# Two ordinary products of each feed-forward replaced by seven block products, in an exact-splitting fp32 transformer kernel

## The chip, the cores and the metric

The kernel runs on one core of one Trainium2 chip. The metric is the device time in microseconds (us). Before the change three runs gave a median of 3119.59 us (3119.15 to 3120.97). The engines are called by the names of the profile: PE (TensorE) multiplies, PEld is its weight load, DVE is VectorE, ACT is ScalarE, POOL is GpSimd and SP is SyncE, which issues the weight transfers.

## The reference, cut to what matters

The program computes two transformer blocks in one launch. The change lies in the second block, which has two layers (`NL` = 2) with two feed-forwards each, so four in all, on 512 tokens plus 16 prefixed ones (`L` = 528 columns):

```python
for l in range(DEPTH_2):
    h = layer_norm(DEEPNORM_ALPHA * h + 0.5 * swiglu_ffn(h, ffn1_w13[l], ffn1_w2[l]), ...)
    mix = token_mix(h, ...)
    h = layer_norm(DEEPNORM_ALPHA * h + mix, ...)
    h = layer_norm(DEEPNORM_ALPHA * h + 0.5 * swiglu_ffn(h, ffn2_w13[l], ffn2_w2[l]), ...)
```

`swiglu_ffn` multiplies the 1024 features of `h` by a gate matrix and an up matrix, forms silu(gate) * up, and multiplies by the down matrix. The computation is in fp32. The last feed-forward needs only the 512 real tokens.

## The kernel before, in words

**Splitting.** An fp32 product is made of three fast ones: weights and activations are each split into a high half and a low half (`w_hi`, `w_lo`, `h_hi`, `h_lo`), and PE forms high x high, high x low and low x high. ACT writes the high half of a weight piece (`split_act`, line 2641), and DVE (line 2659) or POOL (line 2654) the low half, by subtraction. Raw weights come by SP's DMAs into two slots of 4096 columns; the split halves live in a ring of eight "eighths" of 512 columns.

**Tiles.** The hidden width is cut in 22 tiles (f = 0 to 21; the last a half tile), in groups of 6, 8 and 8, each followed by its share of the down product. An ordinary tile makes its gate and its up product whole: eight blocks of 128 features, three pairs, two halves of 264 columns, so 48 matmuls each and 96 a tile. A "seven" tile makes the same four block results from seven block products (Winograd's form of Strassen's scheme) of 4 x 3 = 12 matmuls of 264 columns, so 84 a tile. Its seven weight items are blocks or sums of blocks: item 0 and 5 and 1 come as they are, items 4, 3, 2 and 6 after DVE's weight sums 1 to 4 (`weight_sum_1` to `weight_sum_4`, lines 2679, 2684, 2690, 2696; the first writes the buffer `key_sum`, the others write in place). The low halves of items 0 and 5 are POOL's, the others DVE's. The matching sums of activations are made once in each feed-forward: `hidden_sums` on DVE (four subtractions over 1056 columns, lines 2787 to 2793), their high halves `t_hi` on ACT (line 2804), their low halves `t_lo` on DVE (line 2815).

**A seven tile on PE.** `seven_pe` makes the products 0 to 6 in order, called f.0 to f.6 here. Products 2, 4, 5 and 6 add into a bank that ACT has to copy out first (`kept`, line 2918, signal `sv_sb`); the copies are called kept 1, kept 3, kept 4 and kept 5, after the products whose results they take. Kept 4 stands on ACT behind the high halves of the next tile's items 1, 2 and 3, and item 2's waits for DVE's weight sum 2. The copies go to one half of `gs` or the other.

**The start of a feed-forward.** Before the change tiles 0, 1 and 2 are ordinary and 3 to 20 are sevens. PE makes tile 0's two products and tile 1's gate interleaved with the layer norm (`first_three`), then tile 1's up product, then tile 2. Tile 2's gate product waits only for ACT's silu of tile 0 (line 2991), its up product for DVE's multiplication of tile 0 (line 3085). On ACT, after the layer norm, stand eight scalings of the residual (`scale_res`, line 2608), then the `t_hi` pieces, then two weight pieces, then the silu of tile 0. On DVE stand the hidden sums, `t_lo`, two weight sums for tile 3, then the multiplication of tile 0. Each engine runs its instructions in the order written; semaphores tie the engines together.

Of the kernel before, what the change touches and what calls it, by code (L numbers as in the profile page):

```python
# [2160 lines left out]
def second_block(E):  # L2161
# [739 lines left out]
    def ffn_act(act, l, w):  # L2901
        i = w * S_FFN2
        fin = final(l, w)
        downs = [[i + 6 + 7 * sum(x in F_SEVEN for x in range(f0 + nf)) + (f0 + nf == FT) + DK * g + m for m in range(DK)]
# [63 lines left out]
        for g, (f0, nf) in enumerate(GROUPS):  # L2968
            for f in range(f0, f0 + nf):
# [17 lines left out]
                up_ps.wait(act, l, w * UP + min(2 * f + 1, UP))
                if f >= 2:
                    gl_sb.wait(act, l, n - 1)
                if f < FT - 1:  # L2990
# [830 lines left out]
```

## Time and profile before

| | us |
|---|---|
| median of three runs | 3119.59 |
| the profiled execution | 3117.75 |
| its span, first to last instruction | 3116.0 |
| PE busy | 3024.4 (97%) |
| DVE, ACT, POOL busy | 1627.7, 1139.2, 962.5 |
| mean granted clock of PE | 0.992 |

The span is what the profile divides into parts; the profiled execution took 1.75 us more than it. PE's busy time is a union of matmuls that overlap in the pipeline, so the pace of a stage is read from the chain of waits: a run of matmuls with its length divided by their number.

### The profile page before, as it was taken

How to read it: one execution, taken by the hardware profiler on the slowest of the kernel's cores; microseconds unless marked ns; L12 is line 12 of the kernel's file. 1: busy time of each engine (PE TensorE's matmuls, PEld its weight loads, DVE VectorE, ACT ScalarE, POOL GpSimd, SP SyncE). 2: the span in 40 equal slices, each digit the busy share in tenths (PEclk: the TensorE clock that was granted, in tenths of full speed). 3: DMA queues.
4: the chain of work that ended last, by engine and by line, in shares of the span. 5: the costliest groups of instructions: out<-in, count | busy, mean ns of one | idle time of the engine just before them, and what ended most of it. 6: DMA issues, size and time to landing. Idle time of an engine off the chain costs nothing.

```text
span 3116.0 us, 57215 instructions
## 1 busy us (share of the span) xinstructions
PE 3024.4 (97%) x23846; PEld 2477.9 (80%) x23846; DVE 1627.7 (52%) x2678; ACT 1139.2 (37%) x2208; POOL 962.5 (31%) x699
## 2 busy tenths in 40 slices
PE   7999999989999999999999999999999999999998
PEld 3455578644544438999999999999999999889996
DVE  3143855551122137657464468466575556376573
ACT  2041422110000017445434455356453443364453
POOL 1020266300000004332555432334332356343322
PEclk9999999999999999999999999999999999999999
DMA  7440100139999982332222122231222222113321
GB/s 320 185 169 31 55 3 3 72 139 429 428 429 429 428 350 74 109 109 75 95 82 82 55 75 103 99 112 61 95 109 102 96 82 82 55 60 117 109 75 54
DMA packets 37771, 439.02 MB, mean 141 GB/s; under 512 B 5910, under 2 KB 6678, under 8 KB 11542
## 3 DMA queue, kind: packets, MB, share of 16 engines
q1 hardware_dynamic: 36088, 434.24, 35.5%
q8 instruction: 178, 2.92, 0.4%
q10 hardware_dynamic: 1444, 1.36, 0.1%
q14 instruction: 61, 0.50, 0.0%
HBM read 432.70 MB, written 2.10 MB: 140 GB/s over the span
## 4 chain that ended last, share of the span: by engine, by line
PE 58%; ACT 3%; DVE 1%; issue 0%; DVEq 0%; ACTq 0%
PE PS L2844 23%; PE PS L2712 23%; PE PS L2709 5%; PE PS L2723 2%; PE PS L3240 2%; PE PS L2300 1%; PE PS L3275 1%; PE PS L2306 1%; PE PS L3258 1%; ACT high L2608 0%; ACT h_hi L2522 0%; ACT w_hi L2641 0%; PE PS L2313 0%; ACT low L2525 0%; ACT t_hi L2804 0%
## 5 line engine op out<-in xcount | busy, mean ns | idle before, releaser
L2654 POOL TENSOR_TENSOR w_lo<-low,w_hi 128x512 fp32r<-128x512 f32 (+4 forms) x310 | 616.7, 1995 | 1535.6 <-ACT w_hi L2641 1530.7
L2641 ACT ACTIVATE w_hi<-low 128x512 fp32r<-128x512 f32 (+3 forms) x670 | 491.6, 744 | 502.6 <-PE PS L2712 290.0
L2844 PE MATMUL PS<-t_hi,w_hi 128*128 128x264 f32 (+1 forms) x1152 | 327.1, 284 | 3.8 <-ACT low L2918 3.8
L2844 PE MATMUL PS<-t_hi,w_lo 128*128 128x264 f32 (+1 forms) x1152 | 327.6, 284 | 0.0
L2844 PE MATMUL PS<-t_lo,w_hi 128*128 128x264 f32 (+1 forms) x1152 | 326.2, 283 | 0.0
L2659 DVE TENSOR_TENSOR w_lo<-low,w_hi 128x512 fp32r<-128x512 f32 x360 | 247.0, 703 | 34.2 <-ACT w_hi L2641 33.0
L2844 PE MATMUL PS<-h_hi,w_lo 128*128 128x264 f32 (+1 forms) x864 | 244.9, 283 | 0.0
L2844 PE MATMUL PS<-h_lo,w_hi 128*128 128x264 f32 (+1 forms) x864 | 244.8, 283 | 0.0
L2844 PE MATMUL PS<-h_hi,w_hi 128*128 128x264 f32 (+1 forms) x864 | 244.3, 283 | 0.0
L2712 PE MATMUL PS<-g_hi,w_hi 128*128 128x264 f32 x1056 | 230.9, 286 | 1.2 <-DVE high L3101 1.2
L2712 PE MATMUL PS<-g_lo,w_hi 128*128 128x264 f32 x1056 | 228.6, 284 | 0.0
L1909 PE MATMUL PS<-arena 128*64 128x512 f32 x1024 | 223.1, 593 | 0.3 <-DMA arena<-wts_dram 0.3
L2844 PEld LDWEIGHTS PS<-t_hi,w_hi 128*128 128x128 f32 x1152 | 217.3, 189 | 4.8 <-ACT low L2918 4.6
L2712 PE MATMUL PS<-g_hi,w_lo 128*128 128x264 f32 x1008 | 218.6, 285 | 0.0
L2844 PEld LDWEIGHTS PS<-t_lo,w_hi 128*128 128x128 f32 x1152 | 217.3, 189 | 0.0
L2844 PEld LDWEIGHTS PS<-t_hi,w_lo 128*128 128x128 f32 x1152 | 216.8, 188 | 0.0
L3101 DVE SCALAR_TENSOR_TENSOR high<-PS,high 128x528 f32<-128x528 f32 (+1 forms) x84 | 58.7, 703 | 290.6 <-PE PS L2712 207.8
L2712 PE MATMUL PS<-h_hi,w_hi 128*128 128x264 f32 x928 | 202.9, 289 | 4.6 <-ACT low L2991 4.5
L2712 PE MATMUL PS<-h_hi,w_lo 128*128 128x264 f32 x928 | 200.0, 286 | 0.0
L2712 PE MATMUL PS<-h_lo,w_hi 128*128 128x264 f32 x928 | 199.7, 285 | 0.0
L1909 PEld LDWEIGHTS PS<-arena 128*64 128x64 f32 x1024 | 79.0, 137 | 141.3 <-issue 139.5
L2918 ACT ACTIVATE low<-PS 128x264 f32<-128x264 f32 (+1 forms) x288 | 111.4, 387 | 178.7 <-PE PS L2844 178.0
(435 smaller groups left out, 6543.5 us busy)
## 6 DMA issues: line engine op xcount, KB each, us to landing
arena<-wts_dram SPq DMA_DIRECT2D x108, 2048.0 KB, 18.2
low<-wts_dram SPq DMA_DIRECT2D x70, 2048.0 KB, 7.8
arena<-wmod_dram SPq DMA_DIRECT2D x9, 2048.0 KB, 8.1
low<-wts_dram SPq DMA_DIRECT2D x12, 1536.0 KB, 6.4
arena<-na_bias_dram SPq DMA_DIRECT2D x16, 512.0 KB, 3.6
arena<-x_dram SPq DMA_DIRECT2D x2, 2048.0 KB, 8.2
high<-tab_dram SPq DMA_DIRECT2D x1, 2225.0 KB, 25.2
low<-wts_dram SPq DMA_DIRECT2D x2, 1024.0 KB, 5.5
```

The source lines that it names most:

```text
L1909: last = nc.tensor.matmul(PS[a:b, 2 + 2 * j + half, :], xe[:, k, j * CAP:(j + 1) * CAP], w[:, x, k % 4, :], start=(k == 0), stop=(k == DK ...
L2300: mm = nc.tensor.matmul(PS[32 * j:32 * j + 32, b, at:at + QN], C[mean][:, 0:32], x[:, j * QN:(j + 1) * QN], start=first, stop=last)
L2641: nc.scalar.activation(hi, raw, ACT.Copy).then_inc(w_h.sem, 1)
L2654: nc.gpsimd.tensor_tensor(lo, raw, hi.bitcast(F32), ALU.subtract).then_inc(w_lp.sem, 1)
L2659: nc.vector.tensor_tensor(lo, raw, hi.bitcast(F32), ALU.subtract).then_inc(w_lv.sem, 1)
L2709: mm = nc.tensor.matmul(PS[:, b, :], w[wi], x[xi][:, NMETA:], **ends)
L2712: mm = nc.tensor.matmul(bank(b, h), w[wi], halves(x[xi])[:, h, :], **ends)
L2723: return nc.tensor.matmul(bank(2 * z, h), wts[z][wi][:, k * P:(k + 1) * P], part(x, h), start=first, stop=last)
L2844: last = nc.tensor.matmul(PS[:, b, 0:n], wt[wi][:, k, :], xs[xi], start=(i in (0, 1, 3) and k == 0 and j == 0), stop=(k == 3 and j == 2), ...
L2918: nc.scalar.activation(to, PS[:, 4 * (f % 2) + b, 0:width(fin)], ACT.Copy).then_inc(sv_sb.sem, 1)
L3101: nc.vector.scalar_tensor_tensor(toks(res[:, m, :], fin), sums(2 * (m % apart), fin), 0.5, toks(res[:, m, :], fin), ALU.mult, ALU.add).the ...
L3240: last = nc.tensor.matmul(PS[:, b, 0:256], (h_hi, h_lo)[xi][:, k, s:s + P], wt[wi].rearrange("p (k n) -> p k n", k=DK)[:, k, :], start=(k ...
```

## The change

Tile 2 becomes a seven, so that 19 tiles are sevens (`F_SEVEN` starts at 2). PE's work falls by 12 matmuls in each feed-forward. What goes with it:

- The order on DVE at the start of a feed-forward: weight sums 1 and 3 of the first seven tile stand ahead of the hidden sums. Weight sums 2 and 4, the low halves of tile 2's items and tile 1's multiplication come behind tile 0's.
- The order on ACT: the `t_hi` pieces come first, then items 0 and 1 of tile 2, the silu of tile 0, three of the eight scalings, the high half of tile 0's result. The other five scalings are in tiles 3, 4 (one each) and 5 (three).
- In all seven tiles ACT's silu of the first token half comes after kept 5, no longer between the next tile's items 2 and 3.
- The two halves of `gs` change roles (`kept_1`, `kept_2`), and tile 2's first product waits for the banks of tile 0, so for DVE's multiplication of tile 0 and not only for ACT's silu.

```diff
-F_SEVEN = range(3, FT - 1)
+F_SEVEN = range(2, FT - 1)
...
-    def scale_res(act, l, uu):
+    def scale_res(act, l, uu, ks=range(DK)):
         nc.scalar.drain()
-        for k in range(DK):
+        for k in ks:
             nc.scalar.activation(res[:, k, :], res[:, k, :], ACT.Identity, scale=ALPHA, bias=ashift[:, k:k + 1]).then_inc(ah_sb.sem, 1)
...
-    UP = 7
+    UP = 2 * F_SEVEN[0] + 1
+    kept_1, kept_2 = gs[:, F_SEVEN[0] % 2, :], gs[:, 1 - F_SEVEN[0] % 2, :]
...
+        def gate(f):
+            up_ps.wait(act, l, w * UP + min(2 * f + 1, UP))
+            if f >= 2:
+                gl_sb.wait(act, l, w * FT + f - 1)
+            r = slice(64, 128) if f == FT - 1 else slice(0, 128)
+            nc.scalar.activation(toks(gs[r, f % 2, :], fin), sums(4 * (f % 2), fin)[0:r.stop - r.start], ACT.Silu).then_inc(sl_sb.sem, 1)
...
             if f == F_SEVEN[0]:
+                gl_sb.wait(act, l, w * FT + f - 1)
+                kept(f, 1, kept_1[:, 0:width(fin)], 0)
+                item(f, 4)
+                gate(f - 1)
+                item(f, 5)
+                gate_copy(f - 1, f0)
                 item(f, 6)
-            elif followed:
-                second_half_gate(f - 1, f0)
-            step(0)
-            if f == F_SEVEN[0]:
-                gl_sb.wait(act, l, w * FT + f - 1)
-            kept(f, 1, gs[:, 1, 0:width(fin)], 0)
-            step(1)
-            if followed:
-                gate_copy(f - 1, f0)
-            if f == F_SEVEN[0]:
+                step(0)
                 gl_sb.wait(act, l, w * FT + f)
-            kept(f, 3, gs[:, 0, h0], 0)
+                kept(f, 3, kept_2[:, h0], 0)
+                step(1)
+            else:
+                if followed:
+                    second_half_gate(f - 1, f0)
+                step(0)
+                kept(f, 1, kept_1[:, 0:width(fin)], 0)
+                step(1)
+                if followed:
+                    gate_copy(f - 1, f0)
+                kept(f, 3, kept_2[:, h0], 0)
             step(2)
+            step(3)
+            kept(f, 4, kept_1[:, LH:LH + width(fin)], 1)
+            step(4)
+            kept(f, 5, kept_2[:, h1], 0)
             c11_sb.wait(act, l, seventh(w, f) + 1)
             nc.scalar.activation(g_full(f, f0)[:, h0], g_full(f, f0)[:, h0], ACT.Silu)
-            step(3)
-            kept(f, 4, gs[:, 1, LH:LH + width(fin)], 1)
-            step(4)
-            kept(f, 5, gs[:, 0, h1], 0)
             step(5)
+            if f in range(3, 6):
+                scale_res(act, l, 2 * w - 1, (f,) if f < 5 else range(5, DK))
             step(6)
...
                 if f == 0:
-                    scale_res(act, l, 2 * w - 1)
                     hidden_sums_high(act, l, w, fin)
-                    split_act(act, l, i + 4)
-                    split_act(act, l, i + 5)
+                    item(2, 0)
+                    item(2, 1)
                     if w == 0:
                         nc.scalar.drain()
                         act.dma_start(par, A["par"][l:l + 1, :, :].rearrange("a p n -> (a p) n")).then_inc(par_in.sem, 16)
+                    gate(0)
+                    scale_res(act, l, 2 * w - 1, range(3))
+                    gate_copy(0, f0)
+                    item(2, 2)
+                    item(2, 3)
...
                 if f == 0:
+                    weight_sum_1(dve, l, seventh(w, 2))
+                    weight_sum_3(dve, l, seventh(w, 2))
                     hidden_sums(dve, l, w, fin)
                     hidden_sums_low(dve, l, w, fin)
-                    weight_sum_1(dve, l, seventh(w, 3))
-                    weight_sum_3(dve, l, seventh(w, 3))
                 elif f == 1:
-                    low_item(3, 1)
-                    weight_sum_2(dve, l, seventh(w, 3))
-                    weight_sum_4(dve, l, seventh(w, 3))
-                elif f == 2:
-                    low_item(3, 2, 3, 4)
+                    low_item(2, 3, 4)
```

VectorE (DVE) before, from the last of the hidden sums' low halves (L2815) to tile 1's multiplication (the second L3085); L2679, L2684, L2690 and L2696 are weight sums 1, 3, 2 and 4, L2659 is an item's low half, L3023 the low half of a tile's result:

```order
L2815 TENSOR_TENSOR t_lo<-low,t_hi_7842 128x264
L2679 TENSOR_TENSOR low<-low 128x512 [waits arrived1]
L2684 TENSOR_TENSOR low<-low 128x512 [waits ks_ps0]
L3085 TENSOR_TENSOR low<-low,PS 128x528 [waits x_ps1,xt_ps0]
L3023 TENSOR_TENSOR g_lo<-low,g_hi 128x528 [waits a_ps1]
L2659 TENSOR_TENSOR w_lo<-low,w_hi 128x512 [waits qk_psd1]
L2690 TENSOR_TENSOR low<-low 128x512 [waits ks_ps0,ks_ps1]
L2696 TENSOR_TENSOR low<-low 128x512 [waits ks_ps0,qk_psd0]
L3085 TENSOR_TENSOR low<-low,PS 128x528 [waits x_ps1,xt_ps0]
```

The same stretch after the change, on to weight sum 2 of the next tile (the second L2690); L2816, L3086 and L3028 are the former L2815, L3085 and L3023:

```order
L2816 TENSOR_TENSOR t_lo<-low,t_hi_7842 128x264
L3086 TENSOR_TENSOR low<-low,PS 128x528 [waits x_ps1,xt_ps0]
L2659 TENSOR_TENSOR w_lo<-low,w_hi 128x512 [waits qk_psd1]
L2690 TENSOR_TENSOR low<-low 128x512 [waits ks_ps0,ks_ps1]
L3028 TENSOR_TENSOR g_lo<-low,g_hi 128x528 [waits a_ps1]
L2696 TENSOR_TENSOR low<-low 128x512 [waits ks_ps0,qk_psd0]
L2659 TENSOR_TENSOR w_lo<-low,w_hi 128x512 [waits qk_psd1] x3
L3086 TENSOR_TENSOR low<-low,PS 128x528 [waits x_ps1,xt_ps0]
L2679 TENSOR_TENSOR low<-low 128x512 [waits ks_ps0,qk_psd0,arrived1]
L3028 TENSOR_TENSOR g_lo<-low,g_hi 128x528 [waits a_ps1]
L2659 TENSOR_TENSOR w_lo<-low,w_hi 128x512 [waits qk_psd1]
L2684 TENSOR_TENSOR low<-low 128x512 [waits ks_ps0]
```

The first two weight sums have left this stretch for the place ahead of the hidden sums; the next tile's weight sums 1 and 3 have entered it, since the next tile now follows one tile earlier.

ScalarE (ACT) before, from the end of the layer norm (L2582) to the high half of tile 0's result (L2913); L2608 is a scaling, L2804 a `t_hi` piece, L2641 an item's high half, L2991 the silu of tile 0 with its table load:

```order
L2582 ACTIVATE low<-high 128x8
L2608 ACTIVATE high<-high,low 128x528 x8
L2804 ACTIVATE t_hi_7842<-low 128x1056 [waits d_ps1] x2
L2804 ACTIVATE t_hi_7843<-low 128x1056 [waits d_ps1]
L2804 ACTIVATE t_hi_7843<-low 128x792 [waits d_ps1]
L2804 ACTIVATE t_hi_7842<-low 128x264
L2641 ACTIVATE w_hi<-low 128x1024 [waits xt_ps0,arrived1] x2
L2981 DMA high<-par_dram 128x890
L2991 ACT_TABLE_LOAD
L2991 ACTIVATE low<-PS 128x528 [waits xt_ps0]
L2913 ACTIVATE g_hi<-low 128x528 [waits x_ps0]
```

The same stretch after (L2805, L2997, L2930 and L2914 are the former L2804, L2981, L2991 and L2913):

```order
L2582 ACTIVATE low<-high 128x8
L2805 ACTIVATE t_hi_7842<-low 128x1056 [waits d_ps1] x2
L2805 ACTIVATE t_hi_7843<-low 128x1056 [waits d_ps1]
L2805 ACTIVATE t_hi_7843<-low 128x792 [waits d_ps1]
L2805 ACTIVATE t_hi_7842<-low 128x264
L2641 ACTIVATE w_hi<-low 128x512 [waits xt_ps0,arrived1] x2
L2997 DMA high<-par_dram 128x890
L2930 ACT_TABLE_LOAD
L2930 ACTIVATE low<-PS 128x528 [waits xt_ps0]
L2608 ACTIVATE high<-high,low 128x528 x3
L2914 ACTIVATE g_hi<-low 128x528 [waits x_ps0]
```

The eight scalings have left the head of the stretch; three stand behind the silu. The DMA is only in the first feed-forward of each layer.

## Rows read from the trace of the kernel before

**Rows 1.** The page: busy us (share of the span) and instructions by engine.

```profile
PE 3024.4 (97%) x23846; PEld 2477.9 (80%) x23846; DVE 1627.7 (52%) x2678; ACT 1139.2 (37%) x2208; POOL 962.5 (31%) x699
```

**Rows 2.** PE's waits, 1190 to 3050 us: total us, times, longest us.

```profile
PE PS L2712 <- ACT low L2991: 4.5, 2, 2.5
PE PS L2844 <- ACT low L2918: 3.8, 4, 1.4
...
PE PS L2709 <- ACT low L2991: 2.6, 1, 2.6
```

**Rows 3.** Chain, layer 0's second feed-forward: start us, us, what.

```profile
1802.03 11.96 PE PS L2712 x96
...
1822.66 23.66 PE PS L2844 x192
```

**Rows 4.** The same view, group 2 of that feed-forward.

```profile
1881.33 81.89 PE PS L2844 x672
```

**Rows 5.** The same view, layer 0's first feed-forward.

```profile
1200.21 17.62 PE PS L2712 x144
...
1225.88 14.14 PE PS L2844 x114
```

**Rows 6.** The same view, layer 1's first feed-forward.

```profile
2169.01 13.49 PE PS L2712 x96
...
2190.57 23.68 PE PS L2844 x192
```

**Rows 7.** The same view, layer 1's second feed-forward.

```profile
2766.43 12.94 PE PS L2709 x48
...
2787.35 23.00 PE PS L2844 x192
```

**Rows 8.** VectorE's timeline, as rows 3: start us, us, instruction, [idle before].

```profile
1789.95 1.26 DVE L2787 TENSOR_TENSOR low<-low 128x1056 f32<-128x1056 f32 x1 [2.95 <-POOL h_lo L2590]
...
1795.18 6.98 DVE L2815 TENSOR_TENSOR t_lo<-low,t_hi 128x1056 fp32r<-128x1056 f32 x5
1802.09 2.88 DVE L2679 TENSOR_TENSOR low<-low 128x512 f32<-128x512 f32 x1
```

**Rows 9.** VectorE's timeline, tile 3 of the same feed-forward.

```profile
1814.82 0.70 DVE L3085 TENSOR_TENSOR low<-low,PS 128x528 f32<-128x528 f32 x1
1815.43 1.19 DVE L2679 TENSOR_TENSOR low<-low 128x512 f32<-128x512 f32 x1
...
1818.26 0.68 DVE L2659 TENSOR_TENSOR w_lo<-low,w_hi 128x512 fp32r<-128x512 f32 x1
```

**Rows 10.** GpSimd's (POOL's) timeline, the same feed-forward, 1786 to 1826 us.

```profile
1785.83 4.09 POOL L2590 TENSOR_TENSOR h_lo<-low,h_hi 128x264 fp32r<-128x264 f32 x5
1799.09 5.33 POOL L2654 TENSOR_TENSOR w_lo<-low,w_hi 128x1024 fp32r<-128x1024 f32 x2 [9.17 <-ACT w_hi L2641]
...
1814.78 3.00 POOL L2654 TENSOR_TENSOR w_lo<-low,w_hi 128x512 fp32r<-128x512 f32 x2 [5.90 <-ACT w_hi L2641]
```

**Rows 11.** ScalarE's timeline, the same feed-forward.

```profile
1793.98 4.09 ACT L2804 ACTIVATE t_hi<-low 128x1056 fp32r<-128x1056 f32 x5
...
1799.98 1.28 ACT L2991 ACT_TABLE_LOAD   x1
...
1821.72 0.61 ACT L2641 ACTIVATE w_hi<-low 128x512 fp32r<-128x512 f32 x1
1822.23 0.37 ACT L2918 ACTIVATE low<-PS 128x264 f32<-128x264 f32 x1
```

**Rows 12.** Windows: stretch, its us, busy (x) by engine, clock (PEclk), DMA share, GB/s.

```profile
2169.60:2173.10 3.50, 3.50 (x19) 3.50 (x18) 3.21 (x3) 0.23 (x1) 1.35 (x1) 0.51 0.02 5
```

**Rows 13.** First hidden sum on VectorE in the other three feed-forwards (timeline).

```profile
1192.01 1.26 DVE L2787 TENSOR_TENSOR low<-low 128x1056 f32<-128x1056 f32 x1 [2.95 <-POOL h_lo L2590]
...
2156.51 1.26 DVE L2787 TENSOR_TENSOR low<-low 128x1056 f32<-128x1056 f32 x1 [2.94 <-POOL h_lo L2590]
...
2754.47 1.22 DVE L2787 TENSOR_TENSOR low<-low 128x1024 f32<-128x1024 f32 x1 [2.95 <-POOL h_lo L2590]
```

More of the change, by code:

```diff
@@ L2136 @@
             for c in range(nf // 2):
-                add_chunk([x for f in (f0 + 2 * c, f0 + 2 * c + 1) for x in ([SINGLE] * 2 if f < 3 else [SEVEN] if f in F_SEVEN else [HALF_TILE])])
+                add_chunk([x for f in (f0 + 2 * c, f0 + 2 * c + 1) for x in ([SINGLE] * 2 if f < F_SEVEN[0] else [SEVEN] if f in F_SEVEN else [HALF_TILE])])
             for c in range(DNC):
@@ L2148 @@
 NS = len(PIECES)
-S_FFN = 6 + 7 * NSEVEN + 1 + DK * len(GROUPS)
+S_FFN = 2 * F_SEVEN[0] + 7 * NSEVEN + 1 + DK * len(GROUPS)
 S_MIX = S_FFN
@@ L2871, in ffn_pe @@
                     last.then_inc(up_ps.sem, 1)
-                i += 2 if f < 3 else 1
+                i += 2 if f < F_SEVEN[0] else 1
             ending = g == len(GROUPS) - 1
@@ L2903, in ffn_act @@
         fin = final(l, w)
-        downs = [[i + 6 + 7 * sum(x in F_SEVEN for x in range(f0 + nf)) + (f0 + nf == FT) + DK * g + m for m in range(DK)]
+        downs = [[i + 2 * F_SEVEN[0] + 7 * sum(x in F_SEVEN for x in range(f0 + nf)) + (f0 + nf == FT) + DK * g + m for m in range(DK)]
                  for g, (f0, nf) in enumerate(GROUPS)]
@@ L2981, in ffn_act @@
                         act.dma_start(par, A["par"][l:l + 1, :, :].rearrange("a p n -> (a p) n")).then_inc(par_in.sem, 16)
-                elif f == 1:
-                    item(3, 0)
-                    item(3, 1)
+                    gate(0)
[3 more added lines that the diff above has]
+                    item(2, 3)
                 elif f == FT - 1:
                     split_act(act, l, downs[g][2])
[L2987 to L2990, printed above, removed]
-                    nc.scalar.activation(toks(gs[:, f % 2, :], fin), sums(4 * (f % 2), fin), ACT.Silu).then_inc(sl_sb.sem, 1)
-                else:
-                    nc.scalar.activation(toks(gs[64:128, f % 2, :], fin), sums(4, fin)[0:64], ACT.Silu).then_inc(sl_sb.sem, 1)
-                if f == 2:
-                    item(3, 4)
-                    item(3, 5)
-                if f != 2:
+                    gate(f)
                     gate_copy(f, f0)
-                if f == 1:
-                    item(3, 2)
-                    item(3, 3)
             for x in range(4 if g < len(GROUPS) - 1 else 3, DK):
@@ L3089, in ffn_dve @@
                     nc.vector.tensor_tensor(toks(x[64:128], fin), toks(x[64:128], fin), sums(4, fin)[64:128], ALU.mult).then_inc(g_sb.sem, 1)
-                if f != 2:
+                if f == 0:
+                    low_item(2, 1)
+                    weight_sum_2(dve, l, seventh(w, 2))
+                    gate_low(f, f0)
+                    weight_sum_4(dve, l, seventh(w, 2))
+                    low_item(2, 2)
+                elif f == FT - 1:
                     gate_low(f, f0)
@@ L3187, in second_block @@
             if g == 0:
-                last_product += [(up_ps, w * UP + z + 1) for z in range(6)]
+                last_product += [(up_ps, w * UP + z + 1) for z in range(2 * F_SEVEN[0])]
             last_product += [(sv_ps, 7 * seventh(w, f) + x + 1) for f in range(f0, f0 + nf) if f in F_SEVEN for x in range(7)]
```

8 lines of the change are left out of this document (4 added, 4 removed).

## The prediction, made before the changed kernel ran

> **What bounds the kernel now.** I read the busy line first: PE is busy for 97% of the span [rows 1], so a change pays where it takes matmuls away without making PE wait. The chain of waits then gives PE's true pace. In a stretch without waits 672 matmuls take 81.89 us [rows 4], 0.122 us each, so a seven tile of 84 takes 10.24 us, one of its block products of 12 takes 1.46 us, and an ordinary tile of 96 takes 11.7 us (measured 11.96 with its start [rows 3]). The list of PE's waits shows where PE stands in the feed-forwards. It waits three times for the silu of tile 0 (line 2991), before tile 2: 2.0 and 2.5 us, and 2.6 us in the last feed-forward [rows 2]; layer 0's first has no such wait, since there 144 matmuls run through [rows 5]. And it waits four times, 3.8 us in all, for a copy of line 2918: kept 4 of tile 3, the first seven tile [rows 2]. Everything the change touches lies between those two waits. The timelines of DVE, ACT and POOL there give the durations.
>
> **What is removed.** 12 matmuls in each of four feed-forwards: 12 x 0.122 = 1.46 us each, 5.8 us in all. If nothing else changed, this would be the gain. ACT's eight scalings no longer delay the silu of tile 0; the load of the table and the silu follow the `t_hi` pieces and two weight pieces. Before, ACT ended `t_hi` at 1798.07 [rows 11]; now `t_hi` waits for DVE's sums instead and ends at about 1797.1, and with two pieces of 0.6 us in place of two of 1 us, then 1.28 for the table and 0.6 for the silu, tile 0's silu is ready at 1800.0 instead of 1801.9. But tile 2's first product also needs the bank that DVE's multiplication of tile 0 reads, and that is now the later one.
>
> **The path through DVE, in the second feed-forward of layer 0.**
> 1. DVE sat idle for 2.95 us before the hidden sums, waiting for POOL's `h_lo` pieces [rows 8]. Weight sums 1 and 3 of tile 2 (0.68 us each, as the DVE instruction of the same width in rows 9) go into this hole. They don't come free. Where POOL runs, DVE instructions whose two inputs both lie in SBUF take longer: weight sum 1 of 0.68 us took 1.19 while POOL worked from 1814.78, and 2.88 beside POOL's two wide pieces, ending half a microsecond after one of them ended; the multiplication that reads PSUM took its usual 0.70 in the same place [rows 8 to 10]. So DVE and POOL take turns, and POOL's remaining `h_lo` pieces (4.09 / 5 = 0.8 each) come out late by what the two sums insert beyond POOL's gaps. I take 0.6 us; the ends are 0 and 1.4 (both sums in full). The hidden sums start at 1790.55.
> 2. The four hidden sums take 5.23 us to the start of `t_lo` (1795.18 - 1789.95). `t_lo` took 6.98 [rows 8] with a wait for a wide POOL piece inside; at the hidden sums' pace (1.26 for 1056 columns) it is 5.0 alone. POOL's piece there is now item 0 of tile 2, 1.3 us (3.00 / 2 less its own wait), so 1.2 us of waiting (ends 0 and 1.3). `t_lo` ends at about 1801.8, the multiplication of tile 0 (0.70) at 1802.4, and PE starts tile 2 at 1802.5. Before it was 1802.03. PE's wait grows to 2.5 us.
> 3. From there DVE has no idle time. Until it reaches weight sum 2 of tile 3 it has eight instructions at a pitch of 0.60 (low half of item 1, weight sum 2, tile 0's low half, weight sum 4, three low halves, multiplication of tile 1), to 1807.2; weight sum 1 of tile 3 beside POOL's item 5, 1.3 instead of 0.6; tile 1's low half, 0.6; item 6 beside POOL's item 0 of tile 3, 1.7 instead of 0.6; weight sum 3, item 1, weight sum 2, together 1.9. Sum: 1812.6. Waits of 0.7 and 1.1 for POOL are in it.
> 4. ACT then makes the high halves of items 2 and 3 (0.61, pitch 0.52) and kept 4 (0.37) [rows 11]: 1812.6 + 1.45 = 1814.05. PE starts product 2.5 at 1814.1. Left alone PE would be there at 1802.5 + 5 x 1.46 = 1809.8. It waits 0.1 for item 2's low half, 1.2 for kept 3 (behind the wait for `gs`, 1809.5), and 3.1 for kept 4.
> 5. From 2.5 on PE has two products of tile 2 and tiles 3, 4, 5. Before, the stretch that began at 1822.66 had two products of tile 3 and tiles 4, 5 [rows 3]. So the change of the end is 1814.1 + 10.24 - 1822.66 = +1.7 us. In other words: 1.46 us of matmuls saved, tile 2 begun 0.5 later, and 4.3 us of waiting inside the first seven tile against 1.4 before.
>
> In tile 3 weight sum 2 of tile 4 comes some 4.9 us after the tile's start and kept 4 after 6.4, where PE asks for it after 7.3, so I expect no more waits. The silu moved behind kept 5 helps here by 0.3 and has no other price. The scalings in tiles 3 and 4, one each, of about the 0.6 us of a high half [rows 11], lie beside matmuls. The three in tile 5 delay its high half by about 0.2 us, ahead of the 60 matmuls of the down product that don't need tile 5. SP's next transfer into the slot of tiles 2 and 3 is let go by that chunk's last low half, now no later than before. The other groups keep their order.
>
> **The other feed-forwards**, by the start of the hidden sums [rows 13]. Layer 1's first: same schedule, 366.56 later, 2.5 starts at 2180.7, against 2190.57 [rows 6]: +0.3 (before, it already held a slow stretch, below). Layer 1's second, 964.52 later, 256 columns, so shorter by 0.3 and a tile of 9.96: +0.9 against 2787.35 [rows 7]. Layer 0's first: DVE's multiplication is ready at 1204.4, before PE gets to tile 2 at 1206.1 (48 of the 144 matmuls [rows 5]), so there is no first wait; DVE's path loses about 0.6 where it needs kept 1; 2.5 starts at 1216.8, against 1225.88: +1.1. Sum of the four: +4.0 us.
>
> **The clock.** Where PE waited 2.5 us the granted clock fell to 0.51 from 0.6 us after it resumed, for 3.5 us [rows 12], that is to the 1.2 GHz level; the 96 matmuls then took 13.49 instead of 11.96 [rows 6, 3], so 1.5 us more. After the wait of 2.6 it fell too (12.94 for 48 matmuls of 512 columns [rows 7]); after that of 2.0 it didn't. The new first wait (2.5, three times) may bring it down, but its price goes into the wait for kept 4: 0.35 us at most, 0.5 in all. The new wait for kept 4 is 2.7 to 3.4 us, four times, and behind it PE sets the pace: each fall costs 1.6. I take two of four: 3.3 us. Ends: 0 and 6.4.
>
> The sum is 4.0 + 0.5 + 3.3 = +7.8 us on the profiled execution's 3117.75 us, so 3125.6. The median of the runs is 1.84 above that execution: 3127.4 us.
>
> The Trainium skill, SBUF — State Buffer, section "Who interferes with whom", says that a VectorE instruction with two SBUF inputs contends with a GpSimd instruction that reads SBUF, and that one with at most one such input does not. By that rule, the trace agrees (1.19 against 0.68, and 0.70 for the PSUM reader). It speaks against putting the weight sums beside `h_lo`.
>
> **Rivals.**
> - *Faster: POOL waits, not DVE.* If DVE held the port in back-to-back runs, the 3.6 us of waits in steps 1 to 3 would be gone: 2.5 would start at 1810.5, -1.9 us in this feed-forward, and -3.3, -2.6 and -0.7 in the others, together -8.5: 3111.1. Against it stand rows 8 and 10, where POOL got in between two DVE instructions; for it, that my places for POOL's pieces are estimates. 8%.
> - *The clock holds.* The schedule is right, and the longer waits bring no slow stretch: +4.0 to +4.5, 3123.9. For it: one of the three waits before left the clock up. With partly shorter DVE waits the time comes to lie nearer 3119. Together 32%.
> - *The forecast*, waits and two or three slow stretches: 3125 to 3130. 45%.
> - *DVE stays late into tile 3.* If every turn with POOL costs a full piece of 1.3 us, the path is 1.6 longer in each feed-forward, and kept 4 of tile 3 is waited for as well: +6.4 more, 3133.8. 13%.
> - *Tile 5's three scalings delay the down product.* They would have to eat the slack of 60 matmuls, 7.3 us less some 4 for tile 5's result; from 3 us of lateness on it would cost what goes beyond. 2%, in the range above.
>
> Of this kernel a measurement can tell about 0.2% (6.2 us) from no change: under 3113.4 is faster, over 3125.8 slower. Faster 0.09, the same 0.38, slower 0.53. The range of eight in ten is 3115 to 3134: it leaves out the first rival and the worst of the fourth. The forecast alone would be 3123 to 3130.
>
> **What the profile after would show.** Step 2: PE waits for DVE line 3086, not for ACT's silu, about 2.5 us, before tile 2 in three feed-forwards, and not at all in the first. Step 3: VectorE without idle time from tile 0's multiplication to weight sum 2, and weight sums beside POOL's pieces at 1.2 us and more. Step 4: PE's largest wait is for line 2919 (kept 4 of tile 2), 2.7 to 3.4 us each, 12 to 17 us for that line in all with kept 3, against 3.8 before. Step 5: stretches of 276 matmuls (2.5 to the end of tile 5) starting 8 to 10 us earlier than 1822.66 and its likes. The clock: slow stretches within 1 us after these waits. The prediction is wrong if that line's waits sum to less than 8 us (then the time is below 3119), or if the hidden sums start at the old time.

## The result, and the profile after

The changed kernel took 3127.46 us (median of nine runs, 3124.97 to 3132.75), the kernel before 3118.72 (nine runs, 3115.59 to 3120.97): the ratio is 1.0035, with a 95% interval of 1.0026 to 1.0043, so slower by more than 0.2%. (The ratio is estimated over all the runs; the quotient of the two medians, 1.0028, lies inside the interval.) The prediction said 3127.4 us with slower as the likeliest outcome. The profiled execution took 3126.33 us, its span 3123.4 us at a mean clock of 0.991.

The page's busy line, which answers to [rows 1]: PE's busy time fell by 3.4 us, and DVE's rose by 43.

```profile
PE 3021.0 (97%) x23846; PEld 2476.0 (79%) x23846; DVE 1670.6 (53%) x2726; ACT 1160.5 (37%) x2248; POOL 964.3 (31%) x699
```

The number of matmuls is the same as before. Three feed-forwards have 12 fewer each, but in the last one, with its 512 tokens, 48 matmuls over 512 columns became 84 over 256, which is the work of 42. So there too an eighth of the tile's work is saved, but not 12 instructions.

PE's waits from 1190 to 3060 us, as in [rows 2] (total us, times, longest us):

```profile
PE PS L2845 <- ACT low L2919: 14.1, 7, 2.9
PE PS L2845 <- issue: 4.9, 2, 2.4
...
PE PS L2845 <- DVE low L3086: 2.8, 1, 2.8
```

Line 2919 is `kept`. Its 14.1 us are four waits of 2.75 to 2.93 us for kept 4 of tile 2, and three of 0.66, 0.99 and 1.02 for kept 3; before, this line's waits came to 3.8 us. The two waits put down to "issue" and the one for L3086 are the same wait, before tile 2: DVE's multiplication of tile 0 ended at 1802.35 and PE started at 1802.45. The silu of tile 0 (ended at 1800.09) is waited for no more.

The chain of waits in layer 0's second feed-forward, with [rows 3] (start us, us, what):

```profile
1787.67 2.91 POOL h_lo L2590 x3
1790.60 1.26 DVE low L2788
...
1795.91 4.24 DVE t_lo L2816 x3
...
1801.74 0.61 DVE low L3086
...
1807.20 1.37 DVE low L2679
...
1809.19 1.68 DVE w_lo L2659
...
1812.00 0.69 DVE low L2690
...
1813.33 0.61 ACT w_hi L2641
1813.94 0.29 ACT low L2919
1814.27 35.41 PE PS L2845 x276
```

For the 27 us shown no step of the chain is PE's: POOL's last `h_lo` pieces, then DVE's list from the hidden sums to weight sum 2 (L2690), then ACT, then product 2.5. The timelines give the durations. VectorE's, which answers to [rows 8, 9]:

```profile
1786.95 1.12 DVE L2679 TENSOR_TENSOR low<-low 128x512 f32<-128x512 f32 x1
1788.10 1.13 DVE L2684 TENSOR_TENSOR low<-low 128x512 f32<-128x512 f32 x1
1790.60 1.26 DVE L2788 TENSOR_TENSOR low<-low 128x1056 f32<-128x1056 f32 x1 [1.36 <-POOL h_lo L2590]
...
1795.82 5.92 DVE L2816 TENSOR_TENSOR t_lo<-low,t_hi 128x1056 fp32r<-128x1056 f32 x5
1801.66 0.69 DVE L3086 TENSOR_TENSOR low<-low,PS 128x528 f32<-128x528 f32 x1
...
1807.12 1.45 DVE L2679 TENSOR_TENSOR low<-low 128x512 f32<-128x512 f32 x1
1808.49 0.69 DVE L3028 TENSOR_TENSOR g_lo<-low,g_hi 128x528 fp32r<-128x528 f32 x1
1809.11 1.76 DVE L2659 TENSOR_TENSOR w_lo<-low,w_hi 128x512 fp32r<-128x512 f32 x1
...
1812.00 0.68 DVE L2690 TENSOR_TENSOR low<-low 128x512 f32<-128x512 f32 x1
```

And GpSimd's, with [rows 10]:

```profile
1786.76 3.80 POOL L2590 TENSOR_TENSOR h_lo<-low,h_hi 128x264 fp32r<-128x264 f32 x4 [0.15 <-ACT low L2525]
1797.72 1.67 POOL L2654 TENSOR_TENSOR w_lo<-low,w_hi 128x512 fp32r<-128x512 f32 x1 [7.16 <-ACT w_hi L2641]
1806.72 1.30 POOL L2654 TENSOR_TENSOR w_lo<-low,w_hi 128x512 fp32r<-128x512 f32 x1 [7.34 <-ACT w_hi L2641]
1809.00 1.32 POOL L2654 TENSOR_TENSOR w_lo<-low,w_hi 128x512 fp32r<-128x512 f32 x1 [0.98 <-ACT w_hi L2641]
```

Each of the last three POOL pieces lies beside DVE work that is longer than usual: `t_lo` by 1.1 us (e7 below gives its length alone), weight sum 1 by 0.8 and the low half by 1.1 over the 0.68 of their width. In the last two, DVE's instruction ends 0.55 us after POOL's piece. The first two weight sums, beside `h_lo`, are longer by 0.44. From the start of the hidden sums to weight sum 2 nothing else in DVE's list is longer.

The stretches from product 2.5 to the end of tile 5 in the other three feed-forwards (chain of waits; [rows 5 to 7]):

```profile
1215.62 33.89 PE PS L2845 x276
...
2184.15 35.30 PE PS L2845 x276
...
2783.66 34.45 PE PS L2845 x276
```

In the first three feed-forwards the same 276 matmuls take 33.89 or 35.3 to 35.4 us, and the clock tells them apart. Windows (stretch, its us, busy (x) by engine, clock, DMA share, GB/s): the first around the start of product 2.5 in layer 1's first feed-forward, the second from 0.4 us after that start in layer 0's first:

```profile
2183.90:2187.30 3.40, 3.15 (x14) 3.15 (x15) 2.38 (x6) 1.89 (x6) 1.50 (x1) 0.50 0.01 2
1216.00:1219.50 3.50, 3.50 (x32) 3.50 (x30) 3.39 (x7) 2.48 (x7) 1.52 (x1) 1.00 0.00 0
```

The first row is a slow stretch: 3.4 us at a granted clock of 0.50, the 1.2 GHz level. The second holds 32 matmuls at the full clock, where the first has 14.

Where the time went, counted in each feed-forward from the end of the layer norm on DVE to the end of tile 5 on PE:

| feed-forward | start of 2.5 after the norm | change of tile 5's end | of it a slow stretch |
|---|---|---|---|
| layer 0, first | 27.24 | +0.68 | none |
| layer 0, second | 27.24 | +3.33 | 1.52 |
| layer 1, first | 27.24 | +1.86 | 1.41 |
| layer 1, second | 26.92 | +2.55 | 1.39 |

The slow stretches are priced as 35.41 and 35.30 less 33.89, and the last as 34.45 less 33.06 (276 at the pace of [rows 7]). The sum is +8.4: 4.1 from the schedule and 4.3 from three slow stretches behind 2.5. The span grew by 7.4; the part ahead of these feed-forwards and the part behind tile 5 of the last came out 1.0 shorter in this pair of profiles.

From the end of tile 5 to the end of the last seven tile the first three feed-forwards take 235.3 us before and after alike. So the silu moved behind kept 5 in all sevens, and the three scalings in tile 5, cost nothing that these profiles show.

### The profile page after: what moved, and what is told of

Read it like the earlier page. It is cut to its first block, busy times and chain, and to the rows that moved or that the text cites. A ratio compares the mean times of both kernels' runs of the same rounds, so it can differ in the third digit from the quotient of the medians.

```text
span 3123.4 us, 57359 instructions
## 1 busy us (share of the span) xinstructions
PE 3021.0 (97%) x23846; PEld 2476.0 (79%) x23846; DVE 1670.6 (53%) x2726; ACT 1160.5 (37%) x2248; POOL 964.3 (31%) x699
## 3 DMA queue, kind: packets, MB, share of 16 engines
q1 hardware_dynamic: 36088, 434.24, 35.4%
## 4 chain that ended last, share of the span: by engine, by line
PE 57%; DVE 3%; ACT 1%; issue 0%; POOL 0%; DVEq 0%; ACTq 0%
PE PS L2845 24%; PE PS L2712 21%; PE PS L2709 4%; PE PS L3247 2%; PE PS L2723 1%; PE PS L2300 1%; PE PS L3282 1%; DVE t_lo L2816 1%; PE PS L2306 1%; DVE w_lo L2659 1%; PE PS L3265 1%; ACT h_hi L2522 1%; ACT low L2525 0%; POOL h_lo L2590 0%; PE PS L2313 0%
## 5 line engine op out<-in xcount | busy, mean ns | idle before, releaser
L2641 ACT ACTIVATE w_hi<-low 128x512 fp32r<-128x512 f32 (+3 forms) x690 | 494.6, 735 | 474.6 <-PE PS L2712 286.9
L2845 PE MATMUL PS<-t_hi,w_hi 128*128 128x264 f32 (+1 forms) x1216 | 346.5, 285 | 14.1 <-ACT low L2919 14.1
L2845 PE MATMUL PS<-t_hi,w_lo 128*128 128x264 f32 (+1 forms) x1216 | 346.9, 285 | 0.0
L2845 PE MATMUL PS<-t_lo,w_hi 128*128 128x264 f32 (+1 forms) x1216 | 345.5, 284 | 0.0
L2659 DVE TENSOR_TENSOR w_lo<-low,w_hi 128x512 fp32r<-128x512 f32 x380 | 273.5, 737 | 27.9 <-ACT w_hi L2641 27.1
L2845 PE MATMUL PS<-h_hi,w_hi 128*128 128x264 f32 (+1 forms) x912 | 260.0, 285 | 7.7 <-issue 4.9
L2845 PE MATMUL PS<-h_lo,w_hi 128*128 128x264 f32 (+1 forms) x912 | 260.1, 285 | 0.0
L2845 PE MATMUL PS<-h_hi,w_lo 128*128 128x264 f32 (+1 forms) x912 | 260.0, 285 | 0.0
L2919 ACT ACTIVATE low<-PS 128x264 f32<-128x264 f32 (+1 forms) x304 | 118.0, 388 | 197.2 <-PE PS L2845 193.0
L2712 PE MATMUL PS<-h_hi,w_hi 128*128 128x264 f32 x832 | 182.5, 288 | 0.2
L2845 PEld LDWEIGHTS PS<-h_hi,w_hi 128*128 128x128 f32 x912 | 173.5, 190 | 8.6 <-issue 8.5
L2712 PE MATMUL PS<-h_hi,w_lo 128*128 128x264 f32 x832 | 179.7, 285 | 0.0
```

What stands on the lines that cost most here:

```text
L2641: nc.scalar.activation(hi, raw, ACT.Copy).then_inc(w_h.sem, 1)
L2659: nc.vector.tensor_tensor(lo, raw, hi.bitcast(F32), ALU.subtract).then_inc(w_lv.sem, 1)
L2712: mm = nc.tensor.matmul(bank(b, h), w[wi], halves(x[xi])[:, h, :], **ends)
L2845: last = nc.tensor.matmul(PS[:, b, 0:n], wt[wi][:, k, :], xs[xi], start=(i in (0, 1, 3) and k == 0 and j == 0), stop=(k == 3 and j == 2), ...
L2919: nc.scalar.activation(to, PS[:, 4 * (f % 2) + b, 0:width(fin)], ACT.Copy).then_inc(sv_sb.sem, 1)
```

## The experiments

The theory: the path to product 2.5 is DVE's list with its turns against POOL, then kept 4, which stands on ACT behind weight sum 2; each long wait may also lower PE's clock. The kernel before ran beside each group of experiments, with medians of 3116.4 to 3116.6 us, 2 us less than beside the change, so the ratios are compared: the change stands at 1.0035. The line numbers move a little with each edit; `kept` is L2918 in the kernel before, L2919 in the changed one, L2920 in e12. Starts are counted from the end of the layer norm on DVE, as in the table above. A trace shows one execution of a kernel, and so does each count of slow stretches.

**e1: ACT's scalings alone, in the kernel before.** Three of the eight behind tile 0's silu, one each in tiles 3 and 4, three in tile 5.

```diff
...
+            if f in range(3, 6):
+                scale_res(act, l, 2 * w - 1, (f,) if f < 5 else range(5, DK))
...
                 if f == 0:
-                    scale_res(act, l, 2 * w - 1)
                     hidden_sums_high(act, l, w, fin)
...
+                if f == 0:
+                    scale_res(act, l, 2 * w - 1, range(3))
```

> The kernel before (tile 2 still ordinary) with only the scalings moved: three behind the silu of tile 0, one each in tiles 3 and 4, three in tile 5. Theory (a DVE path with turns against POOL sets the changed kernel's start): here tile 2's first product needs only ACT's silu, which comes at 1800.3 instead of 1801.9 in layer 0's second feed-forward, so PE's three waits of 2.0, 2.5 and 2.6 us before tile 2 shrink to 0.5 or less, and the two slow stretches behind them go: 1.6 to 2 us and 1.5 us of clock twice, some 8 us less than before, 3110 to 3113. The wait for kept 4 of tile 3 stays (3 to 5 us in all). Rival (the moved scalings are themselves a cost, since ACT is late in tiles 3 to 5): no gain or a loss, 3118 to 3123, and more waits for line 2918. Second rival: DVE is what tile 2 really waits for here too (its second product needs the multiplication of tile 0 at 1806.3): the wait moves to DVE and the gain is below 3 us.

Measured: 3118.64 us, ratio 1.0008 [0.9999, 1.0017]. PE's waits:

```profile
PE PS L2844 <- ACT low L2918: 7.5, 6, 2.0
...
PE PS L2712 <- POOL w_lo L2654: 2.1, 2, 1.1
PE PS L2709 <- POOL w_lo L2654: 1.4, 1, 1.4
```

The expectation of a gain missed. In three feed-forwards the wait before tile 2 fell by 1.0 to 1.4 us, and PE now waited for POOL's low half; but the wait for kept 4 of tile 3 grew to 1.93 to 2.01 us, and behind each of these three waits came a slow stretch of 3.4 us. In layer 0's second feed-forward product 3.5 began 35.68 us after the norm, where it began at 35.65 before: weight sum 2 of tile 4 came no earlier. An earlier start of PE is only waiting moved one tile on when DVE's list is the limit.

**e2: the change with all eight scalings at the head of ACT's list again.**

```diff
-            if f in range(3, 6):
-                scale_res(act, l, 2 * w - 1, (f,) if f < 5 else range(5, DK))
...
                 if f == 0:
+                    scale_res(act, l, 2 * w - 1)
                     hidden_sums_high(act, l, w, fin)
...
-                    scale_res(act, l, 2 * w - 1, range(3))
```

> The changed kernel with all eight scalings back at the head of ACT, ahead of the t_hi pieces. Theory: the silu of tile 0 then comes at 1801.1 to 1801.6, still before DVE begins the multiplication of tile 0 at 1801.7, so PE's waits stay as they are (22 us for tiles 2's start and kept 4 together, 2.5 starts within 0.3 us of where it was): within 2 us of the changed kernel, 3125 to 3130. Rival (ACT's order carries the start): tile 2 starts 1 to 2 us later in three feed-forwards and the time is 4 us or more above the changed kernel, over 3131.

Measured: 3127.12 us, ratio 1.0031 [1.0019, 1.0043], as expected, the wait for kept 4 and kept 3 again 14.1 us in 7. In three feed-forwards product 2.5 began within 0.04 us of the table's times. In the change the place of the scalings is worth nothing.

In layer 0's first feed-forward 2.5 began at 28.34, 1.1 us later. There PE came to tile 2 at 17.1 us after the norm, as in the kernel before, and not at 16.0 as in the changed kernel's profile: the last slow stretch before it lasted 10.2 us and not 6.8. Kept 1 waited for PE, the high half behind it for kept 1, and DVE for that high half (ACT's and DVE's timelines):

```profile
1207.90 0.39 ACT L2919 ACTIVATE low<-PS 128x264 f32<-128x264 f32 x1 [0.98 <-PE PS L2845]
1208.84 0.69 DVE L2659 TENSOR_TENSOR w_lo<-low,w_hi 128x512 fp32r<-128x512 f32 x1 [0.77 <-ACT w_hi L2641]
```

**e3: weight sums 1 and 3 behind the hidden sums and `t_lo`.**

```diff
-                    weight_sum_1(dve, l, seventh(w, 2))
-                    weight_sum_3(dve, l, seventh(w, 2))
                     hidden_sums(dve, l, w, fin)
                     hidden_sums_low(dve, l, w, fin)
+                    weight_sum_1(dve, l, seventh(w, 2))
+                    weight_sum_3(dve, l, seventh(w, 2))
```

> The changed kernel with weight sums 1 and 3 of tile 2 behind the hidden sums' low halves, as before the change. Theory: the hidden sums start 0.65 us earlier, the two sums then cost 1.2 us of the path: the multiplication of tile 0 and product 2.5 come 0.5 to 0.6 us later in three feed-forwards and 1.0 to 1.2 in layer 0's first, where the early sums cost nothing; some 3 us more than the changed kernel, 3128 to 3133. Rival (the turns with POOL beside h_lo cost more than the sums give): 2.5 starts earlier and the time falls below 3126.

Measured: 3131.56 us, ratio 1.0047 [1.0033, 1.0060], as expected; the interval overlaps that of the change, so the traces have to tell. PE waits 3.16, 3.16 and 3.52 us before tile 2, and product 2.5 comes 0.7 to 1.6 us later in the four feed-forwards. So the hole in front of the hidden sums is the better place for the two sums, although they don't come free there.

**e4: kept 4 and kept 5 of tile 2 ahead of the high halves on ACT.**

```diff
+            if f == F_SEVEN[0]:
+                kept(f, 4, kept_1[:, LH:LH + width(fin)], 1)
+                kept(f, 5, kept_2[:, h1], 0)
             step(2)
             step(3)
-            kept(f, 4, kept_1[:, LH:LH + width(fin)], 1)
+            if not (f == F_SEVEN[0]):
+                kept(f, 4, kept_1[:, LH:LH + width(fin)], 1)
...
```

> The changed kernel with ACT's kept 4 and kept 5 of tile 2 ahead of the high halves of tile 3's items 2, 3 and 4, so that product 2.5 no longer hangs on weight sum 2 of tile 3. Theory: the wait of 2.9 us before 2.5 goes in all four feed-forwards (2.5 starts at 1811.4 instead of 1814.3), but DVE is late with everything, so a wait of about 2 us comes back before 3.5, where kept 4 of tile 3 hangs on weight sum 2 of tile 4; net 0.8 us each plus one or two fewer slow stretches: 3 to 6 us less than the changed kernel, 3121 to 3125. Rival (the wait was ACT's order alone and DVE has slack): no new wait at 3.5, 2.9 us each and three slow stretches gained, 3110 to 3113.

Measured: 3120.18 us, ratio 1.0012 [1.0003, 1.0021], 0.8 us below the expected range. PE's waits:

```profile
PE PS L2845 <- ACT low L2919: 10.0, 11, 1.3
PE PS L2845 <- issue: 4.9, 2, 2.4
```

The waits of 2.9 us before 2.5 are gone (kept 3's of 0.7 to 1.0 stay), 1.0 to 1.25 us and 0.7 us came in tile 3, and only one slow stretch is left in the four feed-forwards, behind a wait before tile 2. So the wait was the copy's place behind weight sum 2; about two thirds of it came back a tile later.

**e5: the same in tiles 2 and 3.** The condition is `f < F_SEVEN[0] + 2`.

> As e4_kept45_tile2, with kept 4 and kept 5 of tile 3 ahead of tile 4's items too. e4 left per feed-forward a wait of 2.4 before tile 2 (three times), 1.0 in tile 2 and 1.2 + 0.7 in tile 3. Theory (DVE is late with everything in the first sevens, and ACT's order passes that on): the 1.9 in tile 3 goes and at most 1 of it comes back in tile 4, so 4 to 6 us less than e4: 3114 to 3117. Rival (kept 4 and 5 before the items put the items late instead): waits for low halves of items (DVE line 2659) in tile 4, no gain on e4, 3119 or more.

Measured: 3124.50 us, ratio 1.0021 [1.0012, 1.0031]; the expectation missed, and it is no better than e4. PE's waits for `kept` are 12.4 us in 16. ACT's timeline in tile 3 to 4:

```profile
1821.93 0.64 ACT L2914 ACTIVATE g_hi<-high 128x528 fp32r<-128x528 f32 x1 [2.94 <-DVE high L3038]
1822.48 0.65 ACT L2919 ACTIVATE low<-PS 128x264 f32<-128x264 f32 x2
```

Kept 4 and kept 5 of tile 3 (L2919) now stand behind the high half of tile 2's result (L2914), which waits 2.94 us for DVE (L3038). Here the copy that was freed from one wait for DVE stood behind another.

**e6: weight sum 2 of tile 3 two instructions earlier on DVE.**

```diff
             elif f == F_SEVEN[0]:
                 gate_low(f - 1, f0)
+                weight_sum_3(dve, l, s + 1)
+                weight_sum_2(dve, l, s + 1)
                 low_item(f, 6)
-            if not alone:
+                low_item(f + 1, 1)
+            if not alone and f != F_SEVEN[0]:
                 weight_sum_3(dve, l, s + 1)
                 low_item(f + 1, 1)
...
```

> The changed kernel with one order changed on DVE: in tile 2 weight sums 3 and 2 of tile 3 come ahead of item 6 of tile 2 and item 1 of tile 3. Nothing is taken away. Theory (the path to product 2.5 runs through DVE's list to weight sum 2): that list is two instructions shorter, one of which stood beside a POOL piece, and the POOL piece now delays weight sum 3 instead: 2.5 starts 1.2 us earlier (1813.0 in layer 0's second feed-forward), the wait before it is 1.6 to 1.8 instead of 2.9, fewer slow stretches: 4 to 8 us less than the changed kernel, 3119 to 3123. Rival (the wait belongs to PE's late start or to ACT): 2.5 starts where it did, 3125 to 3128.

Measured: 3120.92 us, ratio 1.0018 [1.0009, 1.0027], as expected. In layer 0's second feed-forward the wait before 2.5 fell from 2.88 to 1.87 us, with PE's start of tile 2 unchanged at 15.43 us after the norm (`kept` 9.2 us in 6). Nothing was taken away, and 2.5 came 1.0 us earlier there, 0.4 to 0.7 in the others. This shows that weight sum 2 sets kept 4, and so 2.5.

**e7: POOL only writes.** POOL's subtractions for items 0 and 5 of tile 2 and item 0 of tile 3 are replaced by a fill with zeros of the same buffers.

```diff
+        if PIECES[i % NS][4] in [(w * NSEVEN, 0) for w in range(2)] + [(w * NSEVEN, 5) for w in range(2)] + [(w * NSEVEN + 1, 0) for w in range(2)]:
+            nc.gpsimd.memset(lo.bitcast(F32), 0.0).then_inc(w_lp.sem, 1)
+            return
```

> The changed kernel, but POOL fills three low halves of each feed-forward with zeros in place of the subtraction: items 0 and 5 of tile 2 and item 0 of tile 3. That part of the computation is left out. POOL then reads nothing there. Theory (DVE instructions with two SBUF inputs take turns with POOL's reading): the last pieces of t_lo, weight sum 1 of tile 3 and item 6 of tile 2 take 1.25, 0.68 and 0.68 us instead of 2.34, 1.45 and 1.76; tile 2 starts 1.1 us and product 2.5 some 2.9 us earlier in three feed-forwards and 1 to 2 in the first; with one or no slow stretch left, 9 to 14 us less than the changed kernel, 3113 to 3118. Rival (they take long for another reason, such as data just written by ACT): durations stay, 3125 to 3128.

Measured: 3112.86 us, ratio 0.9990 [0.9981, 0.9999], 0.1 us below the expected range. VectorE's timeline:

```profile
1792.26 4.83 DVE L2819 TENSOR_TENSOR t_lo<-low,t_hi 128x1056 fp32r<-128x1056 f32 x5
...
1802.82 0.68 DVE L2682 TENSOR_TENSOR low<-low 128x512 f32<-128x512 f32 x1
...
1804.23 0.69 DVE L2662 TENSOR_TENSOR w_lo<-low,w_hi 128x512 fp32r<-128x512 f32 x1
```

And GpSimd's:

```profile
1794.14 0.53 POOL L2655 MEMSET w_lo<- 128x512 f32 x1 [7.14 <-ACT w_hi L2641]
```

`t_lo` takes 4.83 us in place of 5.92, weight sum 1 0.68 in place of 1.45, the low half 0.69 in place of 1.76: 1.1, 0.8 and 1.1, the waits for POOL of steps 2 and 3. That is 3.0 us less, but weight sum 2 of tile 3 ends only 2.4 us earlier (23.3 us after the norm instead of 25.7), since DVE now waits 0.26 us for the high half of tile 0's result and stands idle in smaller gaps. So 2.5 comes 1.9 to 2.4 us earlier, not 2.9. PE's first wait becomes 1.3 to 1.7 us, the one before 2.5 1.7, and no slow stretch is left there, where the changed kernel had four. The fills stand in the same places of POOL's list; the first and the third lay beside DVE instructions with two SBUF inputs, and these took their usual time.

**e8: DVE's multiplication of tile 0 ahead of the last `t_lo` piece.** The fourth piece moves behind weight sum 2 of tile 2.

```diff
...
-                    hidden_sums_low(dve, l, w, fin)
+                    hidden_sums_low(dve, l, w, fin, range(3))
...
                     low_item(2, 1)
                     weight_sum_2(dve, l, seventh(w, 2))
+                    hidden_sums_low(dve, l, w, fin, (3,))
```

> The changed kernel with DVE's multiplication of tile 0 ahead of the last of the hidden sums' low halves, which comes behind weight sum 2 of tile 2. DVE's list up to weight sum 2 of tile 3 keeps its length. Theory: tile 2 starts 1.2 us earlier (wait 1.2 instead of 2.4 to 2.8, three times) but product 2.5 starts within 0.3 us of where it did, since the list and not tile 2's start sets it; the wait inside tile 2 grows by the same 1.2, and the time stays within 2 us of the changed kernel: 3125 to 3129. Rival (tile 2's late start on its bank is what costs): 1.2 us three times and its slow stretches gained, 3120 to 3123.

Measured: 3124.13 us (six runs), 0.9 below the expected range, but by its ratio, 1.0032 [1.0020, 1.0044], level with the change. The first wait fell from 2.4 to 2.8 us to between 1.2 and 1.6, but PE waited 1.16 for item 1's low half, and 2.9 before 2.5 as in the change; 2.5 began 0.1 to 0.3 us earlier. PE can start tile 2 earlier: 2.5 comes when DVE's list is through.

**e9: those three low halves on DVE.** `ON_VECTOR` takes items 0 and 5 of tile 2 and item 0 of tile 3 as well; DVE makes item 0 behind `t_lo`, item 5 ahead of item 6, and item 0 of tile 3 ahead of item 1.

> The changed kernel with three low halves of each feed-forward moved from POOL to DVE: items 0 and 5 of tile 2 and item 0 of tile 3. DVE's list is three instructions longer (3 x 0.6 = 1.8 us). Theory: beside those three POOL pieces DVE lost 1.09, 0.77 and 1.08 us, 2.9 in all, so product 2.5 comes 1.1 us earlier although DVE does more; with perhaps one slow stretch fewer 4 to 7 us less than the changed kernel, 3120 to 3123. Rival (DVE's number of instructions is what counts, the turns matter little): 1.8 us later in each feed-forward, 3133 or more.

Measured: 3122.36 us, ratio 1.0019 [1.0010, 1.0028], as expected. VectorE's timeline:

```profile
1795.40 4.83 DVE L2817 TENSOR_TENSOR t_lo<-low,t_hi 128x1056 fp32r<-128x1056 f32 x5
1800.14 0.68 DVE L2660 TENSOR_TENSOR w_lo<-low,w_hi 128x512 fp32r<-128x512 f32 x1
```

The engine that was the limit got three instructions more, and the kernel did not become slower. Product 2.5 began 0.6 to 1.0 us earlier than in the change (1.1 was expected), although five slow stretches lie in these feed-forwards of this profile, one more than in the change. A piece of 512 columns costs DVE 0.60 when it makes it, and 0.8 to 1.1 when POOL makes it beside it.

**e10: kept 4 and kept 5 of tile 3 early, in the kernel before** (the edit of e4, with its buffers).

> The kernel before with one edit: ACT's kept 4 and kept 5 of tile 3 (its first seven tile) ahead of tile 4's items 2 to 4. Theory: PE's wait there (0.8, 1.4, 0.8, 0.9 us) goes, the three before tile 2 (2.0 to 2.6) stay; DVE in the kernel before is less late than in the changed one, so no more than 0.5 us comes back in tile 4: 2 to 4 us less than the kernel before, 3113 to 3115 where the kernel before has 3116.6. Rival (as in e5, all of it comes back one tile later): no gain.

Measured: 3119.08 us, ratio 1.0008 [0.9999, 1.0017]; the expected gain missed. The waits in tile 3 went, and as many came in tile 4 (PE's waits, against 3.8 in 4 before):

```profile
PE PS L2844 <- ACT low L2918: 4.2, 5, 1.0
```

**e11: e1 and e10 together, in the kernel before.**

> The two edits e1 and e10 together on the kernel before. e1 took 1 to 1.5 us off each wait before tile 2 and got it back as 1.9 us before kept 4 of tile 3, with three slow stretches behind it. Theory: without that wait the gain of e1 stays: waits of 1.0 to 1.5 before tile 2, up to 1.2 in tile 4, no slow stretch in the feed-forwards: 5 to 8 us less than the kernel before, 3109 to 3112 where that has 3116.6. Rival (DVE alone sets the pace up to tile 4): within 2 us of the kernel before.

Measured: 3115.80 us, ratio 0.9996 [0.9987, 1.0005]. By its time the rival (within 2 us of the kernel before) was right, although the trace looks as the theory said: PE waits 1.05, 1.06 and 1.46 us before tile 2 and about 1.0 in tile 4, and no slow stretch lies in the four feed-forwards.

**e12: e9 and e4 together.**

> e9 and e4 together on the changed kernel: the three low halves on DVE, and kept 4 and kept 5 of tile 2 early. Theory: e4's 3120.2 less the 1.1 us that DVE's list is shorter, four times, as far as PE waits for that list there (waits of 2.4 before tile 2, 1.0 in it and 1.9 in tile 3 in e4): tile 2 starts 0.5 earlier, the wait in tile 3 is 0.8 to 1.2: 3115.5 to 3118, so about the kernel before. Rival (the waits in tile 3 are not DVE's): within 1 us of e4.

Measured: 3116.20 us, ratio 0.9997 [0.9988, 1.0006], as expected: level with the kernel before and some 0.4% below the change. PE's waits:

```profile
PE PS L2846 <- ACT low L2920: 7.3, 9, 1.1
PE PS L2846 <- DVE low L3093: 6.1, 3, 2.3
```

It still waits 13.4 us in these lines, where the kernel before waits 10.9 in the three of [rows 2]; its span is 1.8 us shorter in the two profiles, where the matmuls saved are worth 5.8. So most of what the seven tile saves is spent. No complete version clearly beat the kernel before.

## Why the prediction was right, point by point

- **Step 1** (the sums delay the hidden sums by 0.6; forecast 1790.55): 1790.60, which is 0.63 later after the norm than before, and 0.62 in layer 0's first feed-forward. The sums took 1.12 and 1.13 us beside `h_lo`, not 0.68.
- **Step 2** (`t_lo` to 1801.8, multiplication 1802.4, PE 1802.5, wait 2.5): 1801.74, 1802.35, 1802.45, wait 2.43. No wait in layer 0's first feed-forward: right.
- **Step 3** (weight sum 2 ends at 1812.6, with waits of 1.2, 0.7 and 1.1 for POOL): 1812.68, with 1.1, 0.8 and 1.1 by the difference to e7 (the first belongs to step 2).
- **Step 4** (2.5 at 1814.1; waits of 1.2 and 3.1): 1814.27; 1.0 and 2.9. `kept` was to be waited for 12 to 17 us in all: 14.1. e6 and e4 show the mechanism, each from one end.
- **Step 5** (+1.7; no waits in tile 3): +1.8 without the clock, and none. In the others +1.1, +0.3 and +0.9 were forecast and +0.7, +0.5 and +1.2 measured. The sum, 4.0, was right to 0.1 us because errors of 0.1 to 0.4 us of both signs cancelled. The term of 0.6 in layer 0's first feed-forward, for DVE waiting there for kept 1, did not appear: 2.5 came 27.24 us after the norm there as elsewhere, since PE came to tile 2 after 16.0 us and not after the 17.0 that the prediction took from the kernel before. The mechanism is real: in e2, where PE came after 17.1, DVE waited 0.77 us and 2.5 came 1.1 us later.
- **The clock** (0.5 for first falls, 3.3 for two falls of four): nothing for the one first fall (layer 1's first feed-forward), 4.3 for three, 1.4 to 1.5 each. The prediction priced a fall at 1.6, although its own rows gave 1.5, and two of them would be 3.2. The number of falls was a guess, and stays one: the same wait, 2.88 and 2.89 us, left the clock up here in layer 0's first feed-forward and was followed by a fall in e2.
- **Luck.** The path was right, the agreement to 0.1 us is chance. The sum said +7.8, and the difference of the medians is +8.7: the kernel before came out 0.9 lower in nine runs than in the three that the prediction started from, and the feed-forwards lost 8.4 instead of 7.8, with one slow stretch behind 2.5 more than forecast.
- **Rivals.** That POOL and not DVE waits is refuted by e7: with the turns away DVE's three stretches are 3.0 us shorter. That each turn costs a full 1.3 us is refuted by the same rows. That the clock holds (3123.9) did not come true in the profiled execution; the other eight have no trace, and the lowest of the nine runs is 3124.97. That tile 5's scalings delay the down product is refuted by the equal times behind tile 5. The scalings' place at the start is worth nothing, as e2 shows.

In my expectations after the prediction I was wrong four times, e1, e5, e10 and, in its main expectation, e11, each time in the same way: I took one wait away and counted it as gained. Three of them show it come back in the next tile. e4, e7 and e8 lay 0.1 to 0.9 us below their ranges. e5 is worse than e4 by 4.3 us in the medians. In the two profiles the spans differ by 2.5 us (3121.2 and 3118.7), which the 2.4 us more waiting for `kept` cover; e5's ten runs range from 3119.31 to 3127.56, and what the rest is stays open.

## What to carry to other kernels

When an engine that feeds the bound one has no idle time in a stretch, a saving on the bound engine there can be worth nothing, as here, until that feeder's list is shorter: follow the list to the instruction that is waited for, and sum it with the turns it takes with its neighbour. Taking away a single wait moved most of it one tile on here; count the gain only after looking what stands next in the queue. A copy that frees a bank should not stand behind work that waits for the late engine, but that alone gives back only part.

## What the runs showed of the hardware

- A GpSimd subtraction that started beside a full VectorE list got in between two instructions: in two of three cases VectorE's next one with two SBUF inputs ended 0.55 us after it. Its 1.3 us cost VectorE 0.8 to 1.1 (1.45 and 1.76 for 0.68, and 1.1 in `t_lo`), and were 1.67 themselves beside `t_lo`. Moving the piece to the saturated engine was no loss (e9).
- A fill by GpSimd (0.53 us for 512 columns), which writes and doesn't read, cost VectorE nothing (e7: 4.83 us for `t_lo` and 0.69 for the low half beside it).
- Idle times of PE of 1.9 to 2.9 us were followed by 3.4 us at the 1.2 GHz level in some cases (1.94 in e1, 2.03 in e10) and not in others (2.03 in the kernel before, 2.88 after the change). In e6 four waits of 1.87 to 1.94 us stood at the same product, and one was followed by a fall. Each fall in a stretch that PE sets costs 1.4 to 1.5 us, as much as the 12 matmuls that a seven tile saves.
